# One 512-column product with the values per attention head, and three reorderings on VectorE, in a hybrid encoder block on Trainium2

## The chip, the cores and the metric

The kernel runs on one core of one Trainium2 chip. The metric is the device time of one execution in microseconds (us). The core has a matrix engine (PE, TensorE), VectorE (DVE), ScalarE (ACT), GpSimd (POOL) and SyncE (SP, which here only starts transfers). Each has its own instruction stream; they meet through semaphores.

## The reference, cut to what matters

One layer, 512 tokens, width 2048, all in float32:

```python
h = _rmsnorm(x, norm_g); proj = h @ w_in            # 2048 x 10304
# branch A: 8 heads, two score matrices per head
s1 = q1 @ k1.T * scale + bias; s2 = q2 @ k2.T * scale + bias
p = softmax(s1) - lam * softmax(s2)                 # 512 x 512 per head
oa = p @ v                                          # 512 x 128 per head
oa = _rmsnorm(oa, a_subln_g, SUBLN_EPS) * (1.0 - lam_init)
ya = (oa * silu(ag)) @ w_oa
# branch B: 8 heads of latent attention with a rotary part
yb = (ob * silu(bg)) @ w_ob
merged = sigmoid(ga) * ya + sigmoid(gb) * yb
out = _rmsnorm(x + merged @ w_out, final_g)
```

The change touches `p @ v` of branch A. Three short edits touch the order of work elsewhere.

## The kernel before, in words

**Split numbers.** Every float32 product is made of three matmuls (`three`): each operand is split into a high part (rounded, by ACT) and a low part (the rest, by DVE), and high by high, high by low and low by high are summed in PSUM. So each tile that PE reads costs one ACT pass (`split_hi`, `merge_hi`, `pt_hi`) and one DVE pass (`split_lo`, `merge_lo`, `pt_lo`) ahead of it.

**Stages.** The first 490 us are 92 *merge steps* (one piece of `w_in` each, in a scheme that trades matmuls for sums of blocks; `merge_sums` on DVE makes the sums of a piece, `merge_lo` its low part). Then come the eight heads of branch A, a stage C (compressed keys and queries, rotary keys, values of B), the eight heads of branch B, the two output projections of the branches, and 24 more merge steps for `w_out` (numbered 92 to 115).

**A head of branch A** is six projection steps `s` of 24 matmuls each (8 tiles `k`, three matmuls a tile), while the attention of the head before is worked off in the gaps. `a_extras(q)` puts that work in: q = 2s in the middle of step s (ahead of tile k = 4), q = 2s + 1 behind step s. Its parts are scores of a tile of 128 queries (`scores_a`), the *turn* of tile t (`turn_p_a`, four transposes of 128 columns into bank `TR`), the product with the values (`pv`), and the sums of squares of the norm (`feature_sums`). Before, the turns of tiles 0 to 3 stand at q = 1, 2, 4 and 6; `pv` of tiles 0 and 1 stands at q = 4 ahead of turn 2, and `pv` of tiles 2 and 3 at q = 7.

**What a turn waits for.** There is one bank `TR`. `turn_p_a(t)` waits for `p_ready` (the probabilities of tile t, the last instruction of `norm_a` on DVE, L1433) and for `pt_lo_ready` of tile t - 1, that is until DVE has read the tile before out of `TR` (`pt_lo`, L1398; ACT's `pt_hi`, L796, comes before it). On DVE the order in step 1 is: low part of a weight piece, `pt_lo(0)`, maxima of tile 2, `pt_lo(1)`, maxima of tile 3, `norm_a(2)`; in step 2: low part of a weight piece, low part of q, `norm_a(3)`, `pt_lo(2)`; in step 3: low part of a weight piece, `pt_lo(3)`. In the first of these rounds (head 0's attention, during head 1's projections) DVE also makes the angles of the rotary tables after steps 2, 3 and 4. After the eighth head the same extras run in stage C with `tail(q)`; there turn 2 is followed by the turns of `c_tok`, which wait for the maxima of all tiles.

**Loops.** Heads 0 and 1 are written out, heads 2 to 7 are a hardware loop of three rounds of two heads; the engines all follow orders written by hand.

## Time and profile before

| | |
|---|---|
| median of 3 runs | 1426.17 us (1425.03 to 1426.52) |
| the profiled execution | 1425.88 us, span 1424.1 us |
| PE busy | 1409.7 us, 99% of the span |
| PE weight loads (beside the matmuls) | 1175.9 us, 83% |
| DVE busy | 1020.1 us, 72% |
| ACT busy | 706.9 us, 50% |
| mean granted TensorE clock | 0.999 |

A matmul's row lasts longer than its place in the stream: rows of 512 columns last 0.39 us, but the next one starts 0.23 us later. So the engine's pace is read from starts, and a wait on PE shows as a start that comes later than that pace.

### The profile page before, as it was taken

What the parts mean: (1) busy time and instruction counts of PE and PEld (TensorE: products, weight loads), DVE (VectorE), ACT (ScalarE), POOL (GpSimd) and SP (SyncE); (2) the same over time, 40 slices, a digit from 0 to 9 for tenths busy, and PEclk for the clock granted to TensorE, in tenths of its full rate; (3) what the DMA queues carried; (4) which work ended last, traced back from release to release, by engine and by line L of the source; (5) the groups of instructions that cost most, each with busy time, mean ns of one, the idle gap of its engine ahead of it and who ended that gap; (6) DMA issues with size and microseconds to landing.
All of it is one profiled execution on the core that took longest, in us unless ns stands there. A gap on an engine that the chain in (4) does not pass through costs nothing.

```text
span 1424.1 us, 17881 instructions
## 1 busy us (share of the span) xinstructions
PE 1409.7 (99%) x6604; PEld 1175.9 (83%) x6604; DVE 1020.1 (72%) x1381; ACT 706.9 (50%) x894; POOL 32.0 (2%) x52
## 2 busy tenths in 40 slices
PE   8999999999999999999999999999999999999997
PEld 7887888888888888888888888888888888888886
DVE  6967888898888868677667665666676354388966
ACT  6546334544344456665666667555564122224434
POOL 0000000000000000000000000000000000000000
PEclk9999999999999999999999999999999999999999
DMA  8449576766756542222222434322342444617674
GB/s 300 146 126 317 176 260 193 232 218 205 246 183 209 186 142 84 80 82 81 81 82 84 114 112 127 88 67 66 85 136 75 156 127 145 207 45 250 201 251 170
DMA packets 182976, 218.43 MB, mean 153 GB/s; under 512 B 19456, under 2 KB 133248, under 8 KB 182272
## 3 DMA queue, kind: packets, MB, share of 16 engines
q1 hardware_dynamic: 174304, 197.64, 44.7%
q10 hardware_dynamic: 8608, 19.93, 3.6%
q8 instruction: 41, 0.67, 0.2%
q14 instruction: 23, 0.19, 0.0%
HBM read 195.51 MB, written 22.02 MB: 153 GB/s over the span
## 4 chain that ended last, share of the span: by engine, by line
PE 91%; DVE 4%; DMA 2%; SPq 1%; ACT 1%; issue 1%; POOL 0%; POOLq 0%; DVEq 0%
PE duo L2118 28%; PE duo L2120 27%; PE duo L2119 27%; PE duo L2171 2%; DMA start_y<-start_columns 1%; PE duo L2148 1%; PE duo L2145 1%; DMA m_raw<-in_w_in_dram 1%; SPq L612 1%; DVE o_lo L1504 1%; PE duo L2162 1%; PE duo L2167 1%; PE duo L2163 1%; PE duo L2166 1%; PE duo L2164 1%
## 5 line engine op out<-in xcount | busy, mean ns | idle before, releaser
L1387 DVE TENSOR_TENSOR w_lo<-w_raw,w_hi 128x1024 fp32r<-128x1024 f32 (+1 forms) x116 | 135.3, 1167 | 100.1 <-ACT w_hi L783 99.5
L2118 PE MATMUL duo<-h_hi,w_hi 128*128 128x512 f32 x512 | 202.3, 395 | 0.0
L2120 PE MATMUL duo<-h_hi,w_lo 128*128 128x512 f32 x512 | 199.7, 390 | 0.0
L2119 PE MATMUL duo<-h_lo,w_hi 128*128 128x512 f32 x512 | 199.6, 390 | 0.0
L888 ACT ACTIVATE m_hi<-m_raw 128x2048 fp32r<-128x2048 f32 (+1 forms) x66 | 115.5, 1752 | 146.8 <-PE duo L2120 75.0
L783 ACT ACTIVATE w_hi<-w_raw 128x1024 fp32r<-128x1024 f32 (+1 forms) x118 | 119.2, 1011 | 124.7 <-DMA w_raw<-in_w_ob_dram 66.0
L1504 DVE TENSOR_TENSOR m_lo<-m_raw,m_hi 128x2048 fp32r<-128x2048 f32 (+3 forms) x71 | 141.9, 2001 | 19.4 <-ACT m_hi L888 19.1
L2118 PE MATMUL duo<-m_hi,h_hi 128*128 128x512 f32 x368 | 143.9, 391 | 2.3 <-DVE m_lo L1504 1.4
L2120 PE MATMUL duo<-m_hi,h_lo 128*128 128x512 f32 x368 | 143.2, 389 | 0.0
L2118 PE MATMUL duo<-m_hi,s_hi 128*128 128x512 f32 x320 | 124.5, 389 | 0.0
L2120 PE MATMUL duo<-m_hi,s_lo 128*128 128x512 f32 x320 | 124.5, 389 | 0.0
L2119 PE MATMUL duo<-m_lo,h_hi 128*128 128x512 f32 x300 | 116.8, 389 | 0.0
L2120 PEld LDWEIGHTS duo<-h_hi,w_lo 128*128 128x128 f32 x512 | 96.1, 188 | 20.5
L2119 PEld LDWEIGHTS duo<-h_lo,w_hi 128*128 128x128 f32 x512 | 96.3, 188 | 18.7
L2118 PEld LDWEIGHTS duo<-h_hi,w_hi 128*128 128x128 f32 x512 | 96.2, 188 | 18.7
L2119 PE MATMUL duo<-m_lo,s_hi 128*128 128x512 f32 x224 | 87.1, 389 | 0.0
L2118 PEld LDWEIGHTS duo<-m_hi,h_hi 128*128 128x128 f32 x368 | 69.1, 188 | 17.7 <-DVE m_lo L1504 2.1
L2120 PEld LDWEIGHTS duo<-m_hi,h_lo 128*128 128x128 f32 x368 | 69.1, 188 | 14.5
L1398 DVE TENSOR_TENSOR pt<-duo,pt 128x512 fp32r<-128x512 f32 x64 | 42.7, 687 | 44.5 <-ACT pt L796 44.3
L1522 DVE TENSOR_TENSOR m_raw<-m_raw 128x512 f32<-128x512 f32 x86 | 56.5, 686 | 19.9 <-DMA m_raw<-in_w_in_dram 19.7
L803 ACT ACTIVATE e<-e,small 128x512 f32<-128x512 f32 x64 | 45.8, 716 | 49.8 <-DVE small L1418 49.8
L2120 PEld LDWEIGHTS duo<-m_hi,s_lo 128*128 128x128 f32 x320 | 60.0, 188 | 12.6
(322 smaller groups left out, 2969.6 us busy)
## 6 DMA issues: line engine op xcount, KB each, us to landing
m_raw<-in_w_in_dram SPq DMA_DIRECT2D x110, 512.0 KB, 4.6
w_raw<-in_w_in_dram SPq DMA_DIRECT2D x132, 256.0 KB, 3.0
o_raw<-in_w_out_dram SPq DMA_DIRECT2D x32, 512.0 KB, 5.0
spare<-in_w_in_dram SPq DMA_DIRECT2D x17, 512.0 KB, 4.8
h_raw<-in_w_in_dram SPq DMA_DIRECT2D x17, 512.0 KB, 5.0
w_raw<-in_w_oa_dram SPq DMA_DIRECT2D x32, 256.0 KB, 3.4
sig<-gates SPq DMA_DIRECT2D x8, 1024.0 KB, 6.2
w_raw<-in_w_ob_dram SPq DMA_DIRECT2D x32, 256.0 KB, 3.4
```

The costliest lines, as they stand in the source:

```text
L612: sp.dma_start(dst, src).then_inc(m_in[st.raw], 16)
L783: act.activation(w_hi[:, piece.slot, 0:cols], w_raw[:, piece.slot, 0:cols], ACT.Copy).then_inc(hi_ready, 1)
L803: last = act.activation(e[:, t % 2, m, :], e[:, t % 2, m, :], ACT.Exp, bias=nm[:, b:b + 1], scale=A_SCALE, accum_out=sums[:, b:b + 1])
L888: act.activation(hi_of(st, 0, st.parts), raw_of(st, 0, st.parts), ACT.Copy).then_inc(m_hi_ready, 1)
L1387: dve.tensor_tensor(w_lo[:, piece.slot, 0:cols], w_raw[:, piece.slot, 0:cols], w_hi[:, piece.slot, 0:cols].bitcast(F32), ALU.subtract).the ...
L1398: dve.tensor_tensor(pt[:, 1, :, c], src[:, :].rearrange("p (k c) -> p k c", k=TOK), pt[:, 0, :, c].bitcast(F32), ALU.subtract).then_inc(pt ...
L1504: dve.tensor_tensor(lo_of(st, p0, p1), raw_of(st, p0, p1), hi_of(st, p0, p1).bitcast(F32), ALU.subtract).then_inc(done, 1)
L1522: dve.tensor_tensor(dst, a, b, ALU.subtract).then_inc(m_first, 1)
L2118: pe.matmul(dst, lhs_hi, rhs_hi, start=start, stop=False)
L2119: pe.matmul(dst, lhs_hi, rhs_lo, start=False, stop=False)
L2120: return pe.matmul(dst, lhs_lo, rhs_hi, start=False, stop=stop)
L2171: last = pe.transpose(dst[:, k * P:(k + 1) * P], src[:, k * P:(k + 1) * P], ident)
```

## The change

The product with the values in branch A is one group of twelve matmuls of 512 columns (`pv_a`, at q = 7), where there were two groups of twelve of 256 (`pv`, at q = 4 and q = 7). For this all four turned tiles of a head stay on chip: the high parts in `pt_hi_whole` (where `pt` was), the low parts in `pt_lo_whole`, which lies over the buffers that the merge stage stored its gates from, so the first low part waits for those stores. ACT's `pt_hi` no longer waits for the first group. `pv_done` counts one per head of A. In step 2 of a head, the extras of q = 4 (now only turn 2) stand ahead of tile k = 5 and not k = 4; in the tail they stay at k = 4. Three places on DVE: merge step 13 and merge step 106 make the low part of the next piece before the sums of the piece after it (they join `LOW_FIRST`), and in B's first head the low part of the rotary query goes before the low part of a weight piece in step 2.

```diff
-LOW_FIRST = [V_STEPS] + FIRST_END[:M_GROUPS] + SECOND_END[:M_GROUPS - 1]
-LOW_FIRST += [OUT0 + L_STEPS + i for i in (0, 1, 2, 4)] + [MID_SPLIT]
+LOW_FIRST = [V_STEPS, V_STEPS + 1] + FIRST_END[:M_GROUPS] + SECOND_END[:M_GROUPS - 1]
+LOW_FIRST += [OUT0 + L_STEPS + i for i in (0, 1, 2, 4)] + [MID_SPLIT, MID_SPLIT + 2]
...
+TURN_2_STEP = 2
...
+        pt_hi_whole = at("pt_hi_whole", 182, [P, TOK, SEQ], F32R)
+        pt_lo_whole = at("pt_lo_whole", 152, [P, TOK, SEQ], F32R)
...
+            def pt_hi_a(head, t):
+                act.wait_ge(p_turned, tile_no(head, t))
+                act.activation(pt_hi_whole[:, :, t * P:(t + 1) * P],
+                               TR[:, :].rearrange("p (k c) -> p k c", k=TOK), ACT.Copy).then_inc(pt_hi_ready, 1)
...
+            def pt_lo_a(head, t):
+                dve.wait_ge(pt_hi_ready, tile_no(head, t))
+                c = slice(t * P, (t + 1) * P)
+                dve.tensor_tensor(pt_lo_whole[:, :, c], TR[:, :].rearrange("p (k c) -> p k c", k=TOK),
+                                  pt_hi_whole[:, :, c].bitcast(F32), ALU.subtract).then_inc(pt_lo_ready, 1)
...
                 if s == 1 and prev:
-                    pt_lo(h - 1, 0, TR)
+                    if first:
+                        for out_n in (g12_out, g22_out):
+                            dve.wait_ge(out_n, 16 * M_GROUPS)
+                    pt_lo_a(h - 1, 0)
...
-                    if s or prev:
+                    if s not in (0, 2) or prev:
                         split_lo(Piece(B0 + s + AHEAD, h, B_STEPS), HALF_PIECE if half else 2 * HALF_PIECE)
                     b_step(s, h, pair, True, prev)
-                    if not s and not prev:
+                    if s in (0, 2) and not prev:
                         split_lo(Piece(B0 + s + AHEAD, h, B_STEPS), HALF_PIECE if half else 2 * HALF_PIECE)
...
+            def pv_a(head):
+                if not isinstance(head, int) or head > 0:
+                    pe.wait_ge(o_copied, head)
+                pe.wait_ge(pt_lo_ready, tile_no(head, TOK - 1))
+                pe.wait_ge(v_lo_ready, head + 1)
+                for k in range(TOK):
+                    last = three(OB[:, :], v_hl[:, 0, k, :], v_hl[:, 1, k, :],
+                                 pt_hi_whole[:, k, :], pt_lo_whole[:, k, :], k == 0, k == TOK - 1)
+                last.then_inc(pv_done, 1)
...
                 if q == 4 and prev:
-                    pv(h - 1, 0, True)
                     turn_p_a(h - 1, 2)
                 if q == 6 and prev:
                     turn_p_a(h - 1, 3)
                 if q == 7 and prev:
-                    pv(h - 1, 1, True)
+                    pv_a(h - 1)
...
-                            lambda: a_extras(2 * s, h, True, prev))
+                            lambda: a_extras(2 * s, h, True, prev), 5 if prev and s == TURN_2_STEP else 4)
```

On PE, in the middle of step 2 of a head (`pt` the turned tiles, `e` the probabilities, `h_hi` by `w_hi` the projection), the kernel before runs

```order
L2118 MATMUL duo<-h_hi,w_hi 128x512
L2119 MATMUL duo<-h_lo,w_hi 128x512
L2120 MATMUL duo<-h_hi,w_lo 128x512
L2118 MATMUL duo<-pt,v_hl 128x256
L2119 MATMUL duo<-pt,v_hl 128x256
L2120 MATMUL duo<-pt,v_hl 128x256
...
L2171 MATMUL duo<-cst,e 128x128 x4
```

and the changed kernel, from tile k = 4 on,

```order
L2137 MATMUL duo<-h_hi,w_hi 128x512
L2138 MATMUL duo<-h_lo,w_hi 128x512
L2139 MATMUL duo<-h_hi,w_lo 128x512
L2190 MATMUL duo<-cst,e 128x128 x4
L2137 MATMUL duo<-h_hi,w_hi 128x512
```

So twelve matmuls of 256 columns are gone ahead of turn 2, and three of the projection have moved ahead of it; between turn 2 and turn 3 stand 21 matmuls of the projection where there were 24.

On DVE around merge step 13 (sums of a piece are the L1522 and L1528 rows, its low part the L1504 row) the order was

```order
L1522 TENSOR_TENSOR m_raw_54<-m_raw_54 128x512
L1528 TENSOR_TENSOR m_raw_54<-m_raw_54 128x512
L1522 TENSOR_TENSOR m_raw_54<-m_raw_54 128x512
L1528 TENSOR_TENSOR m_raw_54<-m_raw_54 128x512
L1504 TENSOR_TENSOR m_lo_55<-m_raw_54,m_hi_66 128x1536
```

and is now

```order
L1538 TENSOR_TENSOR m_raw_54<-m_raw_54 128x512
L1544 TENSOR_TENSOR m_raw_54<-m_raw_54 128x512
L1520 TENSOR_TENSOR m_lo_55<-m_raw_54,m_hi_66 128x1536
L1538 TENSOR_TENSOR m_raw_54<-m_raw_54 128x512
L1544 TENSOR_TENSOR m_raw_54<-m_raw_54 128x512
```

The low part of piece 14 has moved ahead of the sums of piece 15. At merge step 106 the low part of piece 107 moves ahead of the sums of piece 108 in the same way.

On DVE in the first head of B (`rope_in` the rotary query before its split, `qr_hl` its parts) the order was

```order
L1865 TENSOR_TENSOR rope_in_127<-rope_in_127,rope_sw_128 128x512
L1392 TENSOR_TENSOR k_hl_116<-duo0,k_hl_116 128x512
L1387 TENSOR_TENSOR w_lo_74<-w_raw_73,w_hi_75 128x512
L1929 TENSOR_TENSOR qr_hl_137<-rope_in_127,qr_hl_137 64x512
L1387 TENSOR_TENSOR w_lo_74<-w_raw_73,w_hi_75 128x512
```

and is now

```order
L1884 TENSOR_TENSOR rope_in_127<-rope_in_127,rope_sw_128 128x512
L1402 TENSOR_TENSOR k_hl_116<-duo0,k_hl_116 128x512
L1948 TENSOR_TENSOR qr_hl_139<-rope_in_127,qr_hl_139 64x512
L1397 TENSOR_TENSOR w_lo_74<-w_raw_73,w_hi_75 128x512 x2
L1455 TENSOR_REDUCE small_143<-duo1 128x1
```

The low part of the rotary query, which the first scores of B wait for, has moved ahead of one low part of weights.

## Rows read from the trace of the kernel before

**Rows 1.** The page, busy time of the engines.

```profile
PE 1409.7 (99%) x6604; PEld 1175.9 (83%) x6604; DVE 1020.1 (72%) x1381; ACT 706.9 (50%) x894; POOL 32.0 (2%) x52
```

**Rows 2.** Timeline of PE in a loop head: start us, us, engine, line, operation.

```profile
665.38 0.28 PE L2118 MATMUL duo<-pt,v_hl 128*128 128x256 f32 x1
...
666.81 0.60 PE L2171 MATMUL duo<-cst,e 128*128 128x128 f32 x4
...
672.73 0.60 PE L2171 MATMUL duo<-cst,e 128*128 128x128 f32 x4
...
675.92 0.28 PE L2118 MATMUL duo<-pt,v_hl 128*128 128x256 f32 x1
...
684.18 0.39 PE L2118 MATMUL duo<-h_hi,w_hi 128*128 128x512 f32 x1
...
686.90 0.62 PE L2145 MATMUL duo<-ka,qa 128*128 128x512 f32 x2
```

**Rows 3.** Timeline of DVE in the same head.

```profile
664.71 0.75 DVE L1433 SCALAR_TENSOR_TENSOR e<-e,small 128x512 f32<-128x512 f32 x1
...
670.79 0.69 DVE L1398 TENSOR_TENSOR pt<-duo,pt 128x512 fp32r<-128x512 f32 x1
```

**Rows 4.** Timeline around the start of merge step 14.

```profile
111.62 1.49 ACT L888 ACTIVATE m_hi<-m_raw 128x1536 fp32r<-128x1536 f32 x1 [0.46 <-ACT post_p L964]
...
113.95 0.69 DVE L1522 TENSOR_TENSOR m_raw<-m_raw 128x512 f32<-128x512 f32 x1 [5.57 <-DMA m_raw<-in_w_in_dram]
...
115.28 1.75 DVE L1504 TENSOR_TENSOR m_lo<-m_raw,m_hi 128x1536 fp32r<-128x1536 f32 x1
...
115.74 0.39 PE L2120 MATMUL duo<-m_hi,s_lo 128*128 128x512 f32 x1
...
117.09 0.50 PE L2118 MATMUL duo<-m_hi,h_hi 128*128 128x512 f32 x1 [0.96 <-DVE m_lo L1504]
...
117.42 0.39 PE L2119 MATMUL duo<-m_lo,h_hi 128*128 128x512 f32 x1
```

**Rows 5.** Timeline around the first scores of branch B.

```profile
878.43 0.63 ACT L1256 ACTIVATE qr_hl<-rope_in 64x512 fp32r<-64x512 f32 x1 [0.94 <-DVE rope_in L1865]
...
879.61 0.39 PE L2120 MATMUL duo<-h_hi,w_lo 128*128 128x512 f32 x1
...
879.63 0.68 DVE L1929 TENSOR_TENSOR qr_hl<-rope_in,qr_hl 64x512 fp32r<-64x512 f32 x1
...
880.41 0.47 PE L2162 MATMUL duo<-k_hl,q_hl 128*128 128x512 f32 x1 [0.41 <-issue]
```

**Rows 6.** Timeline around the start of merge step 107.

```profile
1341.14 1.29 DVE L1522 TENSOR_TENSOR o_raw<-o_raw 128x512 f32<-128x512 f32 x2
...
1343.07 2.28 DVE L1504 TENSOR_TENSOR mg_lo<-o_spare,o_hi 128x2048 fp32r<-128x2048 f32 x1
...
1344.86 0.39 PE L2120 MATMUL duo<-o_hi,o_s_lo 128*128 128x512 f32 x1
...
1345.41 0.50 PE L2118 MATMUL duo<-o_hi,mg_hi 128*128 128x512 f32 x1 [0.17 <-DVE mg_lo L1504]
```

**Rows 7.** Timeline of the first round: low parts of tiles 2, 3; turn 3.

```profile
546.12 0.69 DVE L1398 TENSOR_TENSOR pt<-duo,pt 128x512 fp32r<-128x512 f32 x1
...
548.05 0.60 PE L2171 MATMUL duo<-cst,e 128*128 128x128 f32 x4
...
549.98 0.68 DVE L1398 TENSOR_TENSOR pt<-duo,pt 128x512 fp32r<-128x512 f32 x1
```

**Rows 8.** Timeline of the last round, in stage C, around its second group.

```profile
837.98 1.06 ACT L783 ACTIVATE w_hi<-w_raw 128x1024 fp32r<-128x1024 f32 x1 [0.84 <-DMA w_raw<-in_w_ukv_dram]
...
839.55 0.69 DVE L1398 TENSOR_TENSOR pt<-duo,pt 128x512 fp32r<-128x512 f32 x1
...
840.30 0.38 PE L2118 MATMUL duo<-pt,v_hl 128*128 128x256 f32 x1
...
841.84 0.40 PE L2118 MATMUL duo<-w_hi,c_hi 128*128 128x512 f32 x1
```

More of the change, by code:

```diff
@@ L794, in pt_hi @@
                 if t >= 2:
-                    act.wait_ge(pv_done, head * 2 + 1)
+                    act.wait_ge(pv_done, head * 2 + (1 - HEADS))
                 act.activation(pt[:, 0, :, (t % 2) * P:(t % 2 + 1) * P],
@@ L822, in v_hi_a @@
                 if not isinstance(head, int) or head > 0:
-                    act.wait_ge(pv_done, head * 2)
+                    act.wait_ge(pv_done, head)
                 act.activation(v_hl[:, 0, :, :], v_raw[:, :, :], ACT.Copy).then_inc(v_hi_ready, 1)
@@ L827, in v_hi_b @@
                 act.wait_ge(v_in, H * 16 + 16)
-                act.wait_ge(pv_done, H * 2)
+                act.wait_ge(pv_done, H * 2 - HEADS)
                 act.activation(v_hl[:, 0, :, :], vb_raw[:, :, :], ACT.Copy).then_inc(v_hi_ready, 1)
@@ L834, in keep_vb @@
                     act.wait_ge(v_in, HEADS * 16)
-                    act.wait_ge(pv_done, HEADS * 2)
+                    act.wait_ge(pv_done, HEADS)
                 if j == TOK:
@@ L1106, in squares @@
             def squares(h):
-                act.wait_ge(pv_done, h * 2)
+                act.wait_ge(pv_done, h)
                 if not isinstance(h, int) or h > 1:
@@ L1127, in a_step @@
                 if s == 1 and prev:
-                    pt_hi(h - 1, 0, TR)
+                    pt_hi_a(h - 1, 0)
                     exp_a(h - 1, 2)
-                    pt_hi(h - 1, 1, TR)
+                    pt_hi_a(h - 1, 1)
                     exp_a(h - 1, 3)
@@ L1139, in a_step @@
                 if s == 2 and prev:
-                    pt_hi(h - 1, 2, TR)
+                    pt_hi_a(h - 1, 2)
                 if s == 3 and prev:
-                    pt_hi(h - 1, 3, TR)
+                    pt_hi_a(h - 1, 3)
                 if s == 4 and cur:
@@ L1321, in _ @@
                 if s == 4:
-                    act.wait_ge(pv_done, 4 * HEADS)
+                    act.wait_ge(pv_done, 3 * HEADS)
                 for head in GATED_AT.get(s, ()):
@@ L1777, in a_step @@
                 if s == 1 and prev:
-                    pt_lo(h - 1, 0, TR)
+                    if first:
+                        for out_n in (g12_out, g22_out):
+                            dve.wait_ge(out_n, 16 * M_GROUPS)
+                    pt_lo_a(h - 1, 0)
                     max_a(h - 1, 2, first)
-                    pt_lo(h - 1, 1, TR)
+                    pt_lo_a(h - 1, 1)
                     if not cur:
@@ L1793, in a_step @@
                     norm_a(h - 1, 3)
-                    pt_lo(h - 1, 2, TR)
+                    pt_lo_a(h - 1, 2)
                 if s == 3 and prev:
-                    pt_lo(h - 1, 3, TR)
+                    pt_lo_a(h - 1, 3)
                 if s == 4 and prev:
@@ L1931, in b_step @@
                 if s == 2 and prev:
-                    dve.wait_ge(pv_done, H * 2)
+                    dve.wait_ge(pv_done, H * 2 - HEADS)
                     dve.wait_ge(acc_read, h * B_READS + (B_READ0 - 2))
@@ L2123, in tile, with project @@
                 return w_hi[:, piece.slot, c0:c0 + width], w_lo[:, piece.slot, c0:c0 + width]
-            def project(piece, dst, half, halves, rhs_hi, rhs_lo, k0, midway=None):
+            def project(piece, dst, half, halves, rhs_hi, rhs_lo, k0, midway=None, midway_at=4):
                 pe.wait_ge(lo_ready, piece.after(0))
                 for k in range(8):
-                    if k == 4 and midway:
+                    if k == midway_at and midway:
                         midway()
@@ L2184, in turn_p_b, with pv @@
                 turn(e_b[:, t % 2, :], SC[t], p_turned)
-            def pv(head, pair, in_a=False):
-                if in_a and pair == 0 and (not isinstance(head, int) or head > 0):
+            def pv_a(head):
+                if not isinstance(head, int) or head > 0:
                     pe.wait_ge(o_copied, head)
+                pe.wait_ge(pt_lo_ready, tile_no(head, TOK - 1))
[4 more added lines that the diff above has]
+                last.then_inc(pv_done, 1)
+            def pv(head, pair):
                 pe.wait_ge(pt_lo_ready, tile_no(head, 2 * pair + 1))
```

## The prediction, made before the changed kernel was run

> **What bounds the kernel now.** I read the page first: PE is busy for 99% of the span and no other engine for more than 72% [rows 1]. So time can come from three places only: fewer or shorter matmuls, waits of PE that are taken away, and against both, waits that are new. The page cannot show short waits, since a matmul's row outlasts its place in the stream. I therefore read the timeline of PE by starts. Twelve projection matmuls of 512 columns take 686.90 - 684.18 = 2.72 us, 0.227 us each; twelve of 256 take 666.81 - 665.38 = 1.43 us, 0.119 us each [rows 2]. Wherever a start comes later than that pace, PE waited, and the timelines of DVE and ACT say for whom.
>
> A wait has a price beyond its length. At merge step 14 DVE's low part ends at 115.28 + 1.75 = 117.03, PE starts at 117.09, and the matmul behind it at 117.42, 0.33 later and not 0.227 [rows 4]. So a matmul released late starts 0.06 us after the end of DVE's row and costs 0.10 us more before the stream has its pace again: 0.16 us behind that end in all. I use this for every wait below; that transposes pay the same 0.10 is an estimate from this row.
>
> **The product itself.** Per head, two groups of 256 columns (1.43 + 1.43) become one of 512 (2.72): 0.14 us less, 1.1 us over eight heads. Columns are the same number; what is saved is the fixed part of twelve matmuls. By 0.227 for 512 and 0.119 for 256 that part is about 11 ns. The Trainium skill, in "TensorE: Matmul & The Clock Gate", section "Back-to-back issue gap", gives an isolated gap of N/2.4 + 2.5 ns, which makes two of 256 only 2.7 ns longer than one of 512. By that rule the 96 pairs would save 0.3 us instead of 1.1. This trace disagrees with it (0.227 us where the rule has 0.216), and I go by the rows.
>
> **Turn 3 in the loop.** In the new order the 1.43 us of the first group are gone ahead of turn 3, and the three projection matmuls moved ahead of turn 2 change nothing here, since they stand ahead of turn 3 both ways. PE would be at turn 3 at 672.73 - 1.43 = 671.30 [rows 2]. But turn 3 needs the bank `TR`, which DVE gives back at the end of tile 2's low part, 670.79 + 0.69 = 671.48 [rows 3]. That end does not come earlier: DVE gets there through a chain that starts at turn 0 (high and low part of tile 0, maxima, ACT's exponentials, a weight piece, q, `norm_a(3)`), and nothing in it waits for the group that is gone. So PE waits, and its stream goes on as if turn 3 had started at 671.48 + 0.16 = 671.64, 0.34 us after 671.30. Net of the 0.14 saved, a loop head is 0.20 us longer: six of them, 1.2 us. Behind PE's wait are only its own projection matmuls; their results have slack on DVE and ACT.
>
> Turn 2 does not wait. It comes at 665.38 + 3 x 0.227 = 666.06, and the probabilities of tile 2 are done at 664.71 + 0.75 = 665.46 [rows 2, 3]. At k = 4 it would have come at 665.38 and waited a little. The one group stands 675.92 - 672.73 = 3.19 us behind turn 3, as the second did, and in the loop the low part of tile 3 has that long, which was enough before.
>
> **The first round.** The same step gives turn 3 at 548.05 - 1.43 = 546.62, tile 2's low part ends at 546.81, so the stream goes on as from 546.97. The group would come 3.19 us later, 550.16. Here DVE has the rotary angles in front of tile 3's low part, which ends at 549.98 + 0.68 = 550.66 [rows 7] and isn't moved by PE. The group goes as from 550.82 and ends at 553.54. Before, it ended at 548.05 + 3.19 + 1.43 = 552.67. So +0.9 us.
>
> **The last round**, in stage C. Its second group already waited: tile 3's low part ends at 839.55 + 0.69 = 840.24 and the group starts at 840.30. That low part is late because ACT made a weight piece first, at 837.98, which had waited for its transfer [rows 8]. SyncE issues that transfer after the maxima of the last tile, so it doesn't move with PE. The 1.43 us that the first group filled are now a wait (for the maxima ahead of the turn of `c_tok`, for tile 2's low part, or for tile 3's), and behind 840.30 stand 0.10 + 2.72 us where there were 841.84 - 840.30 = 1.54. So +1.3 us.
>
> Branch A in all: 1.2 + 0.9 + 1.3 = 3.4 us longer.
>
> **The three orders on DVE.** (1) Merge step 14 should start at 115.74 + 0.23 = 115.97; its stream ran as from 117.42 - 0.23 = 117.19, a loss of 1.22 us. DVE stood idle 5.57 us for the transfer of piece 15, made its sums, and only then the low part of piece 14, whose high part had been ready at 111.62 + 1.49 = 113.11. With the low part first it is done at 113.14 + 1.75 = 114.9, and the whole 1.2 us comes back. The sums of piece 15 now end at 114.9 + 2 x 0.69 = 116.2; with 1.49 for its high part and 1.75 for its low part piece 15 is ready at 119.5, and step 15 starts 24 x 0.227 = 5.4 us after 115.97, at 121.4: 1.9 us of slack [rows 4]. (2) The first scores of B should start at 879.61 + 0.23 = 879.84 and ran as from 880.51. ACT's high part ends at 878.43 + 0.63 = 879.06; with the low part straight behind it, 0.68 us, PE goes as from 879.09 + 0.68 + 0.16 = 879.93. That gives 0.6 and leaves 0.1 [rows 5]. The weight piece that now stands behind is needed a head later. (3) Merge step 107 should start at 1344.86 + 0.23 = 1345.09 and ran as from 1345.51, a loss of 0.4. The low part can go at 1341.14 and ends at 1343.4, so this comes back whole. The sums of piece 108 (some 2 us) then end at 1345.4; with about 2 us on ACT and 2.28 on DVE it is ready at 1349.7, ahead of step 108 at 1345.09 + 5.4 = 1350.5 [rows 6]: 0.8 us of slack. Together 2.2 us less. The new wait for the gate stores I cost at nothing: they are issued by ACT during head 0's projections, and the first low part comes a head later.
>
> **Sum.** 3.4 - 2.2 = +1.2 us on the profiled execution's 1425.88 us is 1427.1. That execution lies 0.29 us under the median, so on the median it would be 1427.4; I say 1427.2. What a measurement of this kernel tells from no change is about 0.2%, 2.85 us, so this is no change.
>
> **Rivals.** (a) DVE is done in time for turn 3. The margin is small (0.18 us by the rows, 0.34 with the price of a wait), so a DVE chain 0.35 us shorter decides it. For it: one weight piece in the chain waits for ACT, and ACT has lost a wait. Against: nothing in the chain was held by the group. In the loop it gives 6 x 0.34 = 2.0 back: 1425.2. If the first and last round also came free, what is left is -1.1 - 2.2 = -3.3, 1422.7, just beyond the bound.
> (b) Slower: the low and high parts now go into rows twice as wide. If each such pass took 0.05 us longer (0.69 now [rows 3]), the five in the chain from turn 0 to tile 2's low part would push it 0.25 us, and with PE waiting there in every round, all eight pay: 2.0 us, 1429.2. From 0.2 us a round on, the kernel is slower by more than the bound. Against: the element count and types are the same.
> (c) The orders give nothing, because the wait moves to the next piece (its sums are what is late): 1425.88 + 3.4 = 1429.3. The slack counted above, 1.9 and 0.8 us, speaks against it.
> (d) The fixed part of a matmul is smaller than the rows show, as when the 256-column groups were slowed by something else. With 3 ns in place of 11 the groups give 0.3 and not 1.1: 1428.0. The skill's rule named above would have it so; the rows bear it out little, as all 24 of a head keep the same pace.
>
> **Numbers.** Forecast, between 1425.8 and 1428.6: 0.68. (a) in the loop alone 0.11, in full 0.09; (b) 0.05, (c) 0.04, (d) 0.03. Faster 0.10, same 0.80, slower 0.10. The range leaves the full (a) and part of the slow cases out: 1424.2 to 1429.0.
>
> **What would show it.** The new profile should show the first matmul of the stream behind turn 3 late in all eight rounds, by about 0.3 us in the loop, with DVE's low part as the one waited for; the group at 0.227 us a matmul; in the first round a second wait of 0.6 us at the group; in stage C the group still starting about 1.3 us after where PE could be, released at the same distance from turn 0; and no late start at merge steps 14 and 107. If turn 3 starts on pace in the loop, the forecast is wrong by 2 us; if DVE's row of the low part is longer than 0.69 us, by up to 2 the other way.

## The result, and the profile after

The changed kernel takes 1429.64 us (median of 10 runs, 1428.39 to 1430.21), the kernel before 1426.10 us (10 runs in the same comparison). The ratio is 1.0027, 95% interval 1.0020 to 1.0035: 3.5 us slower in the medians, where 1.2 us was forecast and the range ended at 1429.0. The profiled execution of the changed kernel is its 1430.03 us one, with a span of 1428.2 us against 1424.1 before.

The page's busy times answer to [rows 1]. TensorE has 96 matmuls fewer (8 heads times 12) and is still at 99%, because a matmul's row outlasts its place:

```profile
PE 1410.3 (99%) x6508; PEld 1170.3 (82%) x6508; DVE 1019.6 (71%) x1381; ACT 706.0 (49%) x894; POOL 32.0 (2%) x52
```

The chain of waits, TensorE alone (engine and line, what it waited for, us in total, times, longest):

```profile
PE duo L2190 <- DVE pt_lo_whole L1408: 1.9, 8, 0.6
PE duo L2137 <- issue: 1.3, 1, 1.3
PE duo L2137 <- ACT vb_keep L853: 1.2, 1, 1.2
...
PE duo L2137 <- DVE pt_lo_whole L1408: 0.4, 1, 0.4
...
PE duo L2489 <- DVE small L1428: 0.3, 1, 0.3
PE duo L2137 <- DVE oT L1838: 0.2, 1, 0.2
```

The first row is turn 3, in all eight rounds. "issue" and the 0.4 of `pt_lo_whole` are the product's group in the last and in the first round. The 0.3 is the first turn of `c_tok`. The rows of `vb_keep` and `oT` are places that the prediction doesn't name at all: the value tiles in stage C and the first projection behind them. In the kernel before no such row stands in this view.

A loop head, timeline of PE (answers to [rows 2]; L2190 is the turn, L2137 to L2139 a triple of matmuls):

```profile
656.53 0.60 PE L2190 MATMUL duo<-cst,e 128*128 128x128 f32 x4
...
671.36 0.39 PE L2139 MATMUL duo<-h_hi,w_lo 128*128 128x512 f32 x1
671.91 0.63 PE L2190 MATMUL duo<-cst,e 128*128 128x128 f32 x4 [0.16 <-DVE pt_lo_whole L1408]
...
672.60 0.39 PE L2138 MATMUL duo<-h_lo,w_hi 128*128 128x512 f32 x1
...
698.25 0.60 PE L2190 MATMUL duo<-cst,e 128*128 128x128 f32 x4
```

and of DVE in it (answers to [rows 3]):

```profile
671.07 0.69 DVE L1408 TENSOR_TENSOR pt_lo_whole<-duo,pt_hi_whole 128x512 fp32r<-128x512 f32 x1
```

Turn 3 could start at 671.36 + 0.227 = 671.59; the low part ends at 671.76 and the turn starts at 671.91. Its four transposes at pace take 0.44 us, so by the start of the second matmul behind it, 672.60, the stream runs as from 672.60 - 0.227 - 0.44 = 671.93: 0.34 us lost. The row's own "0.16" shows less than half of that. The head takes 698.25 - 656.53 = 41.72 us.

The late starts of [rows 4], [rows 5] and [rows 6] are gone. TensorE at merge step 14 and at the first scores of B:

```profile
115.93 0.39 PE L2139 MATMUL duo<-m_hi,s_lo 128*128 128x512 f32 x1
116.15 0.39 PE L2137 MATMUL duo<-m_hi,h_hi 128*128 128x512 f32 x1
...
884.95 0.39 PE L2139 MATMUL duo<-h_hi,w_lo 128*128 128x512 f32 x1
885.17 0.39 PE L2181 MATMUL duo<-k_hl,q_hl 128*128 128x512 f32 x1
```

Each follows its forerunner by 0.22 us, and step 107 does the same at 1349.71 us, 0.23 us behind the matmul ahead of it. The first round (answers to [rows 7]): turn 3 and the group, with the two low parts that they wait for.

```profile
545.15 0.69 DVE L1408 TENSOR_TENSOR pt_lo_whole<-duo,pt_hi_whole 128x512 fp32r<-128x512 f32 x1
...
545.98 0.63 PE L2190 MATMUL duo<-cst,e 128*128 128x128 f32 x4 [0.26 <-DVE pt_lo_whole L1408]
...
549.00 0.68 DVE L1408 TENSOR_TENSOR pt_lo_whole<-duo,pt_hi_whole 128x512 fp32r<-128x512 f32 x1
...
549.74 0.50 PE L2137 MATMUL duo<-pt_hi_whole,v_hl 128*128 128x512 f32 x1 [0.38 <-DVE pt_lo_whole L1408]
```

The last round, in stage C, around the group (answers to [rows 8]):

```profile
840.18 1.06 ACT L788 ACTIVATE w_hi<-w_raw 128x1024 fp32r<-128x1024 f32 x1 [2.25 <-DMA w_raw<-in_w_ukv_dram]
841.14 0.58 ACT L799 ACTIVATE pt_hi_whole<-duo 128x512 fp32r<-128x512 f32 x1
...
841.75 0.69 DVE L1408 TENSOR_TENSOR pt_lo_whole<-duo,pt_hi_whole 128x512 fp32r<-128x512 f32 x1 [1.15 <-ACT pt_hi_whole L799]
...
840.85 0.40 PE L2505 MATMUL duo<-h_hi,w_hi 128*128 128x512 f32 x1
842.54 0.47 PE L2137 MATMUL duo<-pt_hi_whole,v_hl 128*128 128x512 f32 x1 [1.29 <-issue]
```

Last the value tiles of stage C, which no row of before answers to. ScalarE copies each tile of 128 tokens out of its bank (`keep_vb`, L853) and stores it; the fifth tile goes into the room of the first, so its copy waits for all four stores. Timeline of ACT, with the issue of the fourth store (L855), and of PE:

```profile
860.08 0.34 ACTq L855 DMA_DIRECT2D values<-vb_keep  x1
...
864.74 0.60 ACT L853 ACTIVATE vb_keep<-duo 128x512 f32<-128x512 f32 x1 [2.64 <-DMA values<-vb_keep]
...
863.85 0.39 PE L2139 MATMUL duo<-w_hi,c_lo 128*128 128x512 f32 x1
865.39 0.50 PE L2137 MATMUL duo<-w_hi,c_hi 128*128 128x512 f32 x1 [1.16 <-ACT vb_keep L853]
```

The store takes 4.6 us from issue to landing. In the kernel before the same two rows of ACT read:

```profile
856.79 0.34 ACTq L845 DMA_DIRECT2D values<-vb_keep  x1
...
859.39 0.60 ACT L843 ACTIVATE vb_keep<-duo 128x512 f32<-128x512 f32 x1 [0.58 <-DMA values<-vb_keep]
```

2.5 us, and TensorE didn't wait. The DMA view of the stretch from issue to release (queue, kind, packets, MB, share of 16 engines; then the issue with its time to landing) says what is new. The changed kernel, 860.08 to 864.74 us:

```profile
q1 hardware_dynamic: 753, 0.31, 24.7%
q10 hardware_dynamic: 144, 0.26, 15.1%
q8 instruction: 1, 0.02, 1.3%
...
values<-vb_keep ACTq DMA_DIRECT2D x1, 256.0 KB, 4.6
```

The kernel before, 856.79 to 859.39 us:

```profile
q1 hardware_dynamic: 801, 0.32, 46.5%
q10 hardware_dynamic: 144, 0.26, 26.2%
...
values<-vb_keep ACTq DMA_DIRECT2D x1, 256.0 KB, 2.5
```

Nearly the same weight packets (q1) and the same 144 packets of the store (q10) in both; in the changed kernel also one packet of 16 KB, an instruction fetch. It runs from 862.24 for 0.99 us, and from 863.26 to 864.4 us the view has eight packets of the store, one after the other, and nothing else. The view doesn't name the DMA engine of a packet; 144 packets are nine for each of 16 engines, so this fits one engine that had nearly its whole part of the store behind the fetch.

By starts of TensorE's matmuls, each against the same matmul of the kernel before, the span's 4.1 us are: first round +1.0 (0.48 at turn 3, 0.68 at the group, 0.16 saved), loop +1.2 (six waits of 0.34 to 0.43, 0.16 saved in each), last round +2.2 (0.50 at the turn of `c_tok`, 0.77 at turn 3, 1.57 at the group, less 0.46 that stood there before and 0.16 saved), value tiles +2.0, the orders -2.4, and about +0.1 elsewhere (+0.2 at the start of the kernel, where the kernels' single executions differ by up to 1.0 us).

### The profile page after: what moved, and what is told of

It reads as the page before. It is cut to its first block, busy times and chain, and to the rows that moved or that the text cites. A ratio compares the mean times of both kernels' runs of the same rounds, so it can differ in the third digit from the quotient of the medians.

```text
span 1428.2 us, 17666 instructions
## 1 busy us (share of the span) xinstructions
PE 1410.3 (99%) x6508; PEld 1170.3 (82%) x6508; DVE 1019.6 (71%) x1381; ACT 706.0 (49%) x894; POOL 32.0 (2%) x52
## 4 chain that ended last, share of the span: by engine, by line
PE 85%; DVE 5%; ACT 3%; issue 3%; DMA 2%; SPq 1%; POOL 0%; DVEq 0%; ACTq 0%; POOLq 0%
PE duo L2137 26%; PE duo L2139 26%; PE duo L2138 26%; PE duo L2190 2%; DVE e L1428 1%; ACT e L813 1%; PE duo L2164 1%; PE duo L2167 1%; DMA start_y<-start_columns 1%; DVE qa L1808 1%; ACT pt_hi_whole L799 1%; SPq L617 1%; DVE pt_lo_whole L1408 1%; ACT w_hi L788 1%; PE duo L2186 1%
## 5 line engine op out<-in xcount | busy, mean ns | idle before, releaser
L2137 PE MATMUL duo<-h_hi,w_hi 128*128 128x512 f32 x512 | 202.3, 395 | 0.0
L2139 PE MATMUL duo<-h_hi,w_lo 128*128 128x512 f32 x512 | 199.7, 390 | 0.0
L2137 PE MATMUL duo<-m_hi,h_hi 128*128 128x512 f32 x368 | 143.8, 391 | 1.2 <-DVE h_lo L1556 0.8
L2139 PE MATMUL duo<-m_hi,h_lo 128*128 128x512 f32 x368 | 143.2, 389 | 0.0
L2137 PE MATMUL duo<-m_hi,s_hi 128*128 128x512 f32 x320 | 124.5, 389 | 0.0
L2139 PE MATMUL duo<-m_hi,s_lo 128*128 128x512 f32 x320 | 124.5, 389 | 0.0
L2139 PEld LDWEIGHTS duo<-h_hi,w_lo 128*128 128x128 f32 x512 | 96.1, 188 | 20.5
L2137 PEld LDWEIGHTS duo<-h_hi,w_hi 128*128 128x128 f32 x512 | 96.2, 188 | 18.9
L2137 PEld LDWEIGHTS duo<-m_hi,h_hi 128*128 128x128 f32 x368 | 69.1, 188 | 16.3 <-DVE h_lo L1556 1.5
L2139 PEld LDWEIGHTS duo<-m_hi,h_lo 128*128 128x128 f32 x368 | 69.1, 188 | 14.4
L2137 PEld LDWEIGHTS duo<-m_hi,s_hi 128*128 128x128 f32 x320 | 60.1, 188 | 12.5
L2139 PEld LDWEIGHTS duo<-m_hi,s_lo 128*128 128x128 f32 x320 | 60.0, 188 | 12.5
L2137 PE MATMUL duo<-o_hi,mg_hi 128*128 128x512 f32 x176 | 68.6, 389 | 0.0
```

The source lines that it names most:

```text
L2137: pe.matmul(dst, lhs_hi, rhs_hi, start=start, stop=False)
L2139: return pe.matmul(dst, lhs_lo, rhs_hi, start=False, stop=stop)
```

## The experiments

Two theories stood at the start. **Theory 1**: the product costs what its waits show, in the A heads and in stage C, and the orders give what they gave back in the trace. **Theory 2** says where the unforeseen part in stage C comes from: TensorE's program is shorter, so its instruction fetches come at other times, and two of them now lie in transfers that have no slack. Their rivals are in the texts below. All numbers are medians; kernels of one group ran on one chip with the same runs of the kernel before.

### Group 1

The orders alone, on the kernel before:

```diff
-LOW_FIRST = [V_STEPS] + FIRST_END[:M_GROUPS] + SECOND_END[:M_GROUPS - 1]
-LOW_FIRST += [OUT0 + L_STEPS + i for i in (0, 1, 2, 4)] + [MID_SPLIT]
+LOW_FIRST = [V_STEPS, V_STEPS + 1] + FIRST_END[:M_GROUPS] + SECOND_END[:M_GROUPS - 1]
+LOW_FIRST += [OUT0 + L_STEPS + i for i in (0, 1, 2, 4)] + [MID_SPLIT, MID_SPLIT + 2]
...
-                    if s or prev:
+                    if s not in (0, 2) or prev:
```

> The kernel before with only the three orders of VectorE changed; the product stays two groups of 256 columns. Theory 1 (the orders give what the two traces show, late starts of 1.2 us at merge step 14, 0.6 at the first scores of B, 0.4 at merge step 107): 1426.1 - 2.2 = 1423.9 us. Rival (the orders give nothing in the end, because what they gain is lost again behind): 1426.1 us. Further, if the unforeseen waits of TensorE in stage C (864 to 872 us) come from the orders and not from the product, they are here too, and the time is about 1425.9 us with these waits in the trace.

Measured: 1423.64 us against 1425.36, ratio 0.9985 (0.9976 to 0.9994), 1.7 us less. No wait stands at the value tiles. The orders gain, in the medians a little less than the 2.2 us of the forecast; in the trace the three places give back 2.3 us.

The product alone: the changed kernel with these lines as before.

> The changed kernel with the three old orders of VectorE; only the product of the A heads and its parts are new. Theory 1 (the product costs 3.4 us in the A heads as predicted, and about 2 us more by waits in stage C that were not predicted): 1426.1 + 5.7 = 1431.8 us. Rival (the stage C waits come from the orders, or from an accident of when the stage starts, 1.2 us earlier with the orders): 1429.5 to 1430 us and no wait of TensorE at the values of stage C.

Measured: 1431.54 us, 6.2 us above the kernel before, ratio 1.0043 (1.0029 to 1.0057). The chain of waits still has the value tiles, with the same 1.2 us. So these waits belong to the product and not to the orders. The two parts add up: 6.2 - 1.7 = 4.5 us, and the run with the changed kernel's own program in this group (below) lies 4.5 us above the kernel before.

The second four value tiles get other room, idle there (the A keys' and the exponentials'), so the fifth copy waits for no store:

```diff
+        vb_more = [at(f"vb_more{i}", kb, [P, SEQ]) for i, kb in enumerate((164, 166, 174, 176))]
...
-                if j == TOK:
-                    for out_n in v_out:
-                        act.wait_ge(out_n, 32 + 32)
...
-                act.activation(vb_keep[:, t, :], SC[2 + j % 2][:, :], ACT.Copy).then_inc(v_kept, 1)
+                kept = vb_more[t][:, :] if g else vb_keep[:, t, :]
+                act.activation(kept, SC[2 + j % 2][:, :], ACT.Copy).then_inc(v_kept, 1)
```

> The changed kernel, with other room for the second four value tiles of stage C (the room of the A keys and exponentials, idle then), so that ScalarE's copy of tile 4 no longer waits for the four stores of the first tiles. Theory 1 (TensorE's waits of 1.4 us at 864 to 866 us, and those at 868 and 871 us behind them, are that wait for a store, which landed 4.6 us after its issue and in the kernel before 2.5 us): 1429.6 - 1.9 = 1427.7 us, no wait at 864 to 872 us. Rival (these waits have another source, such as a weight piece or VectorE's turn for oT): the waits stay, 1429.3 to 1429.6 us.

Measured: 1428.21 us, 2.9 us above the kernel before and 1.6 below the changed kernel's program in this group. The rows of `vb_keep` and `oT` are gone from the chain of waits, the others stayed. The store was the cause of these waits.

Empty instructions at the start of TensorE's program, to move its fetches:

```diff
+            for _ in range(72):
+                pe.nop(nofuse=True)
             pe.wait_ge(cst_in, 16)
```

> The changed kernel with 72 empty instructions at the start of TensorE's program, as many as its program is shorter by ahead of stage C (36 matmuls and their weight loads), put where it waits for its first load. They compute nothing and only shift where in time TensorE's instruction fetches of 16 KB fall. Theory 2 (the late store in stage C is caused by the fetch at 862.3 us, which held one DMA engine for 0.99 us in front of its packets): the fetch moves to about 854 us, the store lands after 2.5 to 3 us, 1427.7 to 1428.2 us. Rival A (the store is late because it is issued beside weight loads that the later work of the last A head moved up against it): the waits stay, 1429.6 us. Rival B (the fetches, moved, fall on another transfer without slack): waits of about the same size at another place of stages A to C, in the trace behind a fetch.

Measured: 1429.82 us. This tested nothing: the page counts 17666 instructions, as many as for the changed kernel, and TensorE's first matmul starts at 2.78 us as there (2.72), so the empty instructions without a semaphore are not in the program that runs. It is a second measurement of the changed kernel, on this group's chip: 4.5 us above the kernel before.

### Group 2

Empty instructions again, this time meant for stage C, and again not in the program (17666 instructions):

> The changed kernel with 4 empty instructions behind each of the 16 triples of matmuls of stage C's first two steps, 64 in all: they compute nothing, stand where TensorE later waits anyway (832 to 843 us), and shift the fetch behind them by 64 instructions, 32 matmuls and their weight loads, 7.3 us. Theory 2 (the store of value tile 3 in stage C lands 4.6 us after its issue because TensorE's instruction fetch of 16 KB at 862.3 us lies in front of its packets): the fetch comes at about 855 us, the store lands in 2.5 us, the waits at 864 to 872 us are gone, and the kernel is 1.6 us above the kernel before in place of 3.5. Rival (the store is late from the two weight pieces issued 1.3 to 3 us ahead of it, as in the kernel before, or from the later start): the waits stay, 3.5 us above. If empty instructions cost TensorE time that no wait covers, up to 1 us is to be added to both.

Measured: 1429.53 us, 3.6 us above the kernel before. It is the changed kernel in this group. Its three profiled executions have the store landing 4.6, 4.4 and 4.1 us after its issue.

Turn 3 one tile of the projection later in the A heads:

```diff
-                            lambda: a_extras(2 * s, h, True, prev), 5 if prev and s == TURN_2_STEP else 4)
+                            lambda: a_extras(2 * s, h, True, prev),
+                            5 if prev and s in (TURN_2_STEP, TURN_2_STEP + 1) else 4)
```

> The changed kernel with turn 3 of the A heads one tile of the projection later (behind k = 4 instead of ahead of it), 0.68 us. Theory 1 (the wait of 0.35 to 0.49 us there for VectorE's low part of tile 2 is the whole cost in the loop): six rounds gain 2.3 us together, the round ahead of the loop nothing since its wait at the group grows by what turn 3 gains, and the kernel is 1.2 us above the kernel before in place of 3.5. Rival (the low part of tile 3 becomes late for the group instead, since turn 3 is now 0.07 to 0.3 us later in time): a wait at the group of 0.1 us or more in each round, and a gain under 1 us.

Measured: 1427.19 us, ratio 1.0007 (0.9998 to 1.0016), 1.3 us above the kernel before and 2.3 below the changed one, as theory 1 has it. Timeline of PE and DVE in a loop head:

```profile
671.02 0.39 PE L2139 MATMUL duo<-h_hi,w_lo 128*128 128x512 f32 x1
671.25 0.60 PE L2190 MATMUL duo<-cst,e 128*128 128x128 f32 x4
...
672.52 0.69 DVE L1408 TENSOR_TENSOR pt_lo_whole<-duo,pt_hi_whole 128x512 fp32r<-128x512 f32 x1 [0.62 <-ACT pt_hi_whole L799]
...
673.77 0.39 PE L2137 MATMUL duo<-pt_hi_whole,v_hl 128*128 128x512 f32 x1
```

Turn 3 starts on pace, and the low part of tile 3 is done at 673.21, 0.56 us ahead of the group. The head has 696.90 - 655.53 = 41.37 us. The single times lie between 1425.44 and 1428.10, 2.7 us apart, where those of the next two kernels lie 1.3 and 1.0 us apart (but those of the changed kernel's program in the first group 2.8). In the profiled execution, one of 1425.91 us, the store landed in 2.5 us and TensorE didn't wait for it. A fetch lay in this stretch too, but came when all but three packets of the store had been moved.

ScalarE's order in step 3 of stage C, the high part of tile 3 ahead of the weight piece:

```diff
-                if s == VB_STEP:
+                if s in (VB_STEP - 1, VB_STEP):
                     a_step(s, Head(HEADS, C0), False, True)
                 split_hi(Piece(C0 + s + AHEAD), HALF_PIECE if s == C_STEPS - 1 else 2 * HALF_PIECE)
-                if s < VB_STEP:
+                if s < VB_STEP - 1:
```

> The changed kernel with ScalarE's order in step 3 of stage C exchanged: the high part of probability tile 3 ahead of the weight piece, which waits for its transfer until 840.1 us. Theory 1 (the group of the last A head waits 1.57 us since ScalarE stands at that transfer with the high part behind it): the high part is done at about 839.9 us, the low part goes behind three parts of c at 840.6 us and ends at 841.3 us, the group waits 0.4 us, a gain of 1.1 us: 2.4 us above the kernel before in place of 3.5. Rival (the group's wait is not what sets the end of this stage, since the waits behind it grow): no gain, or waits at 864 to 872 us longer by as much.

Measured: 1428.73 us, 2.8 us above the kernel before, 0.8 below the changed one. The high part comes at 839.24 in place of 841.14 us, and the group waits 0.33 us in place of 1.57:

```profile
839.24 0.60 ACT L799 ACTIVATE pt_hi_whole<-duo 128x512 fp32r<-128x512 f32 x1 [1.52 <-PE duo L2190]
...
841.10 0.47 PE L2137 MATMUL duo<-pt_hi_whole,v_hl 128*128 128x512 f32 x1
```

Of the 1.2 us at the group 0.8 reach the end; the waits at the value tiles stayed.

The first part of the rotary angles on VectorE behind the low part of tile 3, in the round ahead of the loop:

```diff
-                    if first and 2 <= s < 5:
-                        rope_angles(s - 2)
+                    for part in {3: (0, 1), 4: (2,)}.get(s, ()) if first else ():
+                        rope_angles(part)
```

> The changed kernel with the first part of the rotary angles on VectorE, in the round ahead of the loop, behind the low part of probability tile 3 instead of ahead of it; four operations, 2 us. Theory 1 (the wait of 0.68 us at the group of this round is those angles): it is gone, the wait of 0.48 us at turn 3 stays, and the kernel is 2.8 us above the kernel before in place of 3.5. Rival (the weight piece in front of the low part is what is late): the wait at the group stays above 0.4 us.

Measured: 1429.31 us, 3.4 us above the kernel before: 0.2 below the changed one, where 0.7 was expected. The group starts on pace (549.41 behind 549.18), so the angles were its wait. But 0.26 us come back at the sums of squares, whose low part VectorE now makes later (554.98 behind 554.62). The rest of the miss is within the spread of the runs.

### Group 3

Empty instructions that stay, since each adds to a semaphore that nobody waits for:

```diff
+            def empty(n):
+                for _ in range(n):
+                    pe.nop(nofuse=True).then_inc(passed_by, 1)
+
+            empty(48)
             pe.wait_ge(cst_in, 16)
...
+            empty(24)
             pe.wait_ge(x_normed, 1)
```

> The changed kernel with 72 empty instructions in TensorE's program ahead of its first matmul and behind its first warm-up, where it waits for loads. Each adds 1 to a semaphore that nobody waits for, which keeps it in the program. They compute nothing and shift the later instructions by what the change took out ahead of stage C. Theory 2 (in stage C the fetches of 16 KB at 836.8 and 862.3 us hold one DMA engine for 0.92 and 0.99 us and make the last packet of a weight piece and of a store late): the fetches come at about 830 and 854 us as in the kernel before, the weight piece is whole at 839.0 in place of 840.2 us and the group of the last A head starts 1.2 us earlier, the store lands in 2.5 us and the waits of 1.9 us at 864 to 872 us are gone: 0.4 us above the kernel before in place of 3.5. Rival (piece and store are late for another reason): 3.5 us above, with the waits where they were. At the start of the kernel the empty instructions may cost up to 1 us, which is to be added to both.

Measured: 1433.05 us, 7.1 above the kernel before. The page has 17738 instructions, 72 more. The first matmul starts at 8.26 in place of 2.72 us: the start was far more expensive than I had allowed for, and 4.0 us of it are still there at merge step 13. What it tells stands in stage C. ACT's timeline at value tiles 3 and 4:

```profile
864.08 0.60 ACT L854 ACTIVATE vb_keep<-duo 128x512 f32<-128x512 f32 x1
864.71 0.34 ACTq L856 DMA_DIRECT2D values<-vb_keep  x1
...
867.38 0.60 ACT L854 ACTIVATE vb_keep<-duo 128x512 f32<-128x512 f32 x1 [0.64 <-DMA values<-vb_keep]
```

and the DMA view from 864.71 to 867.38 us:

```profile
values<-vb_keep ACTq DMA_DIRECT2D x1, 256.0 KB, 2.6
```

There is no fetch in it, and the store lands in 2.6 us. At tile 3 this kernel is 864.08 - 859.45 = 4.6 us behind the changed one, at tile 4 867.38 - 864.74 = 2.6, and its span is 1430.9 - 1428.2 = 2.7 us longer. So shifting the program, with the same work, transfers and waits, takes the 2.0 us away. The fetch has moved into the store of value tile 1, issued at 857.21 us, and that is now the late one. The DMA view from 857.0 to 859.0 us:

```profile
q8 instruction: 1, 0.02, 6.1%
...
values<-vb_keep ACTq DMA_DIRECT2D x1, 256.0 KB, 4.5
```

In the changed kernel this store lands in 2.0 us. Nobody waits for it this early, so it costs nothing. In the last round nothing improved: the weight piece kept ScalarE waiting 2.66 us. There the fetch, against my expectation, came only 2 us earlier among the transfers and not 8, and still lay among them (1.2 us behind the issue of the fourth piece, 3.3 in the changed kernel).

Turn 3 later with these empty instructions:

> The changed kernel with turn 3 a tile later and the 72 empty instructions. With turn 3 alone the times of single executions lay between 1425.4 and 1428.1 us, wider than for any other kernel here, and its profiled one had the store landing in time. Theory 2 (the spread is whether the fetch meets the store): with the shift the spread is 1 us, like that of the others, and the median 1.9 us below the kernel before: 3.5 - 2.3 - 1.2 - 1.9. Rival: the spread stays 2.7 us and the median 1.2 us above the kernel before.

Measured: 1430.79 us (1430.63 to 1431.69 in five runs). The median has the costly start in it. Taking that as in the run above, 1433.05 - 1430.79 = 2.3 us for turn 3, as without the shift. The spread is 1.1 us in place of 2.7, as theory 2 expects, but over five runs, and the kernel before alone spreads over 2.6 us in the comparison with the changed one, so the spread shows little. Its trace shows more: the store of value tile 3 lands in 2.6 us with no fetch in it, and that of tile 1 in 4.3 us with one.

The four edits together, without empty instructions:

> The changed kernel with the four edits of the runs before together: turn 3 a tile later, ScalarE's high part of tile 3 ahead of the weight piece in stage C, the rotary angles behind the low part in the round ahead of the loop, and other room for the second four value tiles. Theory 1 (the waits at turn 3, at the two groups and at the value tiles are the whole cost of the product, and they are independent): 2.3 + 1.1 + 0.5 + 1.6 = 5.5 us less than the changed kernel, 1424.1 us where the kernel before has 1426.1, 2.0 us below it. Rival (the waits are links of one chain, so that mending one lengthens another): 1 us below the kernel before or nothing, with a wait of 0.5 us or more at a place that had none.

Measured: 1424.63 us, ratio 0.9991 (0.9982 to 1.0000), 1.3 us below the kernel before. The span is 5.4 us shorter than that of the changed kernel, the 5.5 of theory 1, but the medians lie 0.7 us less far below the kernel before than expected. In the chain of waits there still stand 0.6 us at the sums of squares of the first round (for `vT_lo`) and 0.6 at turn 3 in the last (for `pt_lo_whole`), where the first turn of `c_tok` waits 0.3 us as well. The rounds at the two ends keep costing, and the orders alone are better.

### Group 4

The one product only in the loop, with turn 3 later; two groups of 256 columns over the whole tiles in the first and last round; ScalarE's order and the other room as above:

```diff
+            def pv_half(head, pair):
+                if pair == 0 and (not isinstance(head, int) or head > 0):
+                    pe.wait_ge(o_copied, head)
+                pe.wait_ge(pt_lo_ready, tile_no(head, 2 * pair + 1))
+                pe.wait_ge(v_lo_ready, head + 1)
+                c = slice(pair * 2 * P, (pair + 1) * 2 * P)
+                for k in range(TOK):
+                    last = three(OB[:, c], v_hl[:, 0, k, :], v_hl[:, 1, k, :],
+                                 pt_hi_whole[:, k, c], pt_lo_whole[:, k, c], k == 0, k == TOK - 1)
```

> One product of 512 columns only in the six rounds of the loop, with turn 3 a tile later; in the round ahead of it and in stage C two groups of 256 columns again, which read the whole tiles. The three orders as changed, and the two robust edits of stage C (ScalarE's order, other room for the second four value tiles). Theory 1 (the product itself is worth 0.14 to 0.16 us a head wherever nothing waits, and the rounds at the ends cost more than they give): 0.9 us below the orders alone, 1425.9 - 1.8 - 0.9 = 1423.2 us. Rival (in sum the product is worth nothing even in the loop, and the orders are the whole gain): as the orders alone, 1424.1 us.

Beside it the kernel before with the three orders, ScalarE's order and the other room, whose diffs stand above, and nothing of the product:

> The kernel before with the three orders and the two edits of stage C (ScalarE's order, other room for the second four value tiles), the product in two groups of 256 columns everywhere. Theory 1 (these two edits give something only where the product or a fetch has made a wait): the last group waits 0.2 us less at most, 1424.0 us, and the one before differs from this by the product in the loop alone. Rival (they gain by themselves): 1423 us or less, and the product in the loop has no part in what the other kernel gains.

Measured: 1423.71 us with the product in the loop, ratio 0.9988 (0.9979 to 0.9997); 1424.20 us without it, ratio 0.9991 (0.9982 to 1.0000); the kernel before has 1425.47 in this group. So the product in the loop is worth 0.5 us of the 0.9 expected. One loop head of the first kernel, from turn 0 to turn 0:

```profile
655.07 0.60 PE L2189 MATMUL duo<-cst,e 128*128 128x128 f32 x4
...
696.44 0.60 PE L2189 MATMUL duo<-cst,e 128*128 128x128 f32 x4
```

and of the second:

```profile
654.88 0.60 PE L2170 MATMUL duo<-cst,e 128*128 128x128 f32 x4
...
696.41 0.60 PE L2170 MATMUL duo<-cst,e 128*128 128x128 f32 x4
```

41.37 against 41.53 us: 0.16 a head, six heads 1.0 us. It is given back in part in stage C, where TensorE waits at the sums of squares in both kernels and not in the one with the orders alone; the row of the first kernel, where the second has 0.60:

```profile
843.69 0.50 PE L2235 MATMUL duo<-vT_hi,ones_sq 128*128 128x512 f32 x1 [0.86 <-DVE vT_lo L1817]
```

By starts it costs 0.9 us in the first and 0.7 in the second. In the second, ScalarE's new order is the likely reason: the weight piece landed at 836.62 us, but ScalarE stood at the high part of tile 3, which waits for turn 3, and split the piece from 837.68 us on, so that the rotary tables and the squares behind it came later too. In the first, the piece itself landed only at 837.46 us. Neither edit of stage C was run alone on two groups, so this stays argued.

These two kernels also show what a fetch does to the weight pieces in the last round. Their last rounds are alike, two groups and the same two edits, but in the first a fetch starts at 834.74 us, among the packets, and in the second none does. The fourth piece takes 6.9 us from issue to landing in the first and 5.6 in the second (DMA view, 830.6 to 830.9 and 831.05 to 831.3 us):

```profile
w_raw<-in_w_ukv_dram SPq DMA_DIRECT2D x1, 256.0 KB, 6.9
...
w_raw<-in_w_ukv_dram SPq DMA_DIRECT2D x1, 256.0 KB, 5.6
```

By their ratios to the kernel before, the orders alone (0.9985) and the loop alone (0.9988) are the best of these kernels and can't be told apart. Both take 1.7 to 1.8 us less than the kernel before, with intervals that end below 1.

## Why the prediction was wrong

**The product itself** was right: 0.14 us a head forecast, 0.16 measured where nothing waits. Rival (d), a smaller fixed part, is out. Out too is what the Trainium skill's rule in "TensorE: Matmul & The Clock Gate", section "Back-to-back issue gap", which is stated for an isolated matmul, would have given: by it two of 256 columns are 2.5 ns longer than one of 512 (the prediction has 2.7), an estimate of 0.03 us a head. This trace disagrees with it.

**Turn 3 in the loop** was right. The low part ends 671.76 - 656.53 = 15.23 us behind turn 0, before 671.48 - 656.26 = 15.22. The loss is 0.34 to 0.43 us a round where 0.34 was forecast; the sum over the loop is 1.2 us as forecast, and taking the wait away gave 2.3 us. Rival (a) is out. Rival (b) is out too: the low part's row is 0.69 us long, as in [rows 3].

**The first round**: 1.0 us for 0.9, with both waits where they were forecast.

**The orders**: 1.7 us in the medians (2.3 and 2.4 in the two traces) for 2.2, all three late starts gone. Rival (c) is out.

**The last round** is the first step that failed. It said that the second group's release "doesn't move with PE", since ScalarE's weight piece stays where it is from turn 0, and gave 1.3 us. The piece came 1.2 us later from turn 0 and the round cost 2.2. The 0.84 us that ScalarE had waited for that transfer before [rows 8] became 2.25, so this transfer had no slack, and I had taken its landing as fixed. That ScalarE stood there with the high part behind it is shown (its order exchanged, the group's wait fell from 1.57 to 0.33 us). Why the transfer was later, the traces of all the kernels here say together: the fourth of these weight pieces took 5.6 us from issue to landing in the three without a fetch among its packets (the kernel before, the orders alone, the second of group 4) and 6.7 to 7.1 us in the other twelve, which all have one (the changed kernel at 836.75 us, for 0.92 us). No edit was made that moves this fetch and nothing else.

**The sum** is the second. It ended with branch A "in all" and had no term for what a shorter program of TensorE does behind it. The value tiles cost 2.0 us, more than half of the whole result, by one store that landed 4.6 us after its issue and not 2.5. That it is the store is shown (other room: 1.6 us less). That its lateness is the place of the instruction fetch is shown by the shifted program, which has the same work and a store of 2.6 us, and another store late with the fetch in it. The other traces agree: this store took 3.9 to 4.7 us in seven kernels, each with a fetch 1.2 to 2.3 us behind its issue, and 2.4 to 2.7 us in eight, of which six have none in it and two have one 2.1 us behind the issue, when only three and six of its packets had still to start. Without these 2.0 us the changed kernel would stand at about 1427.6 us, inside the range.

The product, the loop, the first round and the orders came out as forecast; the 0.9 us of the last round and the 2.0 us of the value tiles are the miss. The range missed for the same reason. Its upper end, 1429.0, was worked out from the waits of one chain, and nothing in it stood for a transfer that another engine's program can delay.

## What to carry to other kernels

Work that is taken out of the bounding engine pays only where what it stood in front of is ready early. Two groups in a head were also 1.4 us of cover for turn 3, and the bank came back 0.2 us too late; one tile later it was on time. Look for that before merging two pieces of work: find who is waited for next, and by how much it is early.

Where an engine waits for a transfer with less than about 2 us of slack (4.6 us in place of 2.5 here), a shorter or longer program elsewhere can make it late. Count such waits on their own, and give the buffer another room or move the wait behind work that others need.

An edit that takes a wait away on one engine moves the order there for all that follows. ScalarE's new order gained 1.2 us at the group; where the group no longer needed it, TensorE waited at the sums of squares, most likely by this order (0.7 us).

## What the hardware showed that I had not expected

Instruction fetches stand among the transfers: one packet of 16 KB each, 0.92 and 0.99 us long in the two places above. Packets of a store came behind it, so that a transfer of 256 KB took 4.6 us and not 2.5, though the DMA engines as a whole were idle for most of the last 2 us.

In the second and third round of the loop over the A heads no fetch of 16 KB stands in the trace of the changed kernel: the DMA view has none between 642 and 836 us. Such fetches start again behind the loop, and 72 more instructions in TensorE's program brought the second of them 8.6 us earlier against the work around it, the first only 2.

Whether fetch and store meet may differ from run to run: the kernel with turn 3 later had single times from 1425.4 to 1428.1 us. Only one of these executions has a trace, so this is not shown.

An empty instruction that adds to a semaphore costs TensorE more than I thought: 48 of them ahead of the first matmul moved its start from 2.72 to 8.26 us, so at least 5.5 / 48 = 0.12 us each.
